# Queueing the first projection of each later stage inside the modulation loop, with split-weight refills one at a time behind it

## The reference

```python
def modulate(x, g, shift, scale):
    return rms_norm(x, g) * (1.0 + scale[:, None, :]) + shift[:, None, :]

# first block: attention + mLSTM, then a mixture of 32 experts
# second block, for i in range(2):
h = rmsnorm(x, norm1_g[i]) * (1.0 + scale1) + shift1
y = diff_attention(h, ...) if i == 0 else axial_gqa(h, ...)   # begins with h @ w_qkv
x = x + gate1 * y
h = rmsnorm(x, norm2_g[i]) * (1.0 + scale2) + shift2
x = x + gate2 * swiglu(h, f_w_in[i], f_w_out[i])              # begins with h @ w_in
```

## Time and profile before

| | us |
|---|---|
| median of 3 runs | 1378.43 (1378.06 to 1382.33) |
| profiled execution | 1377.22 |
| its span, first to last instruction | 1375.4 |
| TensorE busy | 1153.6 (84%) |
| VectorE busy | 611.5 (44%) |
| ScalarE busy | 540.8 (39%) |

### The profile page before, as it was taken

How to read it: one execution, slowest core, us unless ns; L and a number is a source line. 1 busy time by engine, 2 the same in 40 slices (tenths; PEclk the granted TensorE clock), 3 DMA queues, 4 the chain that set the end, 5 groups by cost and what they waited for, 6 DMA issues and landing times.

```text
span 1375.4 us, 22370 instructions
## 1 busy us (share of the span) xinstructions
PE 1153.6 (84%) x9627; PEld 917.0 (67%) x9627; DVE 611.5 (44%) x1363; ACT 540.8 (39%) x1203; POOL 0.2 (0%) x4
## 2 busy tenths in 40 slices
PE   6989998857475666657589989999999989999997
PEld 4867678534243443424257757999998758899997
DVE  4564664201110110101165765665555855655554
ACT  4554553211101111101155665555554654655553
POOL 0000000000000000000000000000000000000000
PEclk9999998989788889978899999999999999999999
DMA  9895847899999999999978655555546655655520
GB/s 390 345 356 223 355 186 294 341 427 427 428 426 426 424 427 427 426 426 428 426 299 307 235 194 198 231 184 184 185 153 230 228 215 184 245 184 184 184 93 31
DMA packets 29569, 397.53 MB, mean 289 GB/s; under 512 B 3480, under 2 KB 4888, under 8 KB 5400
## 3 DMA queue, kind: packets, MB, share of 16 engines
q1 hardware_dynamic: 29032, 395.72, 72.1%
q10 hardware_dynamic: 432, 0.30, 0.1%
HBM read 394.97 MB, written 1.05 MB: 288 GB/s over the span
## 4 chain that ended last, share of the span: by engine, by line
PE 61%; DMA 20%; DVE 10%; ACT 7%; issue 2%; SPq 0%; ACTq 0%; DVEq 0%
PE ps L141 61%; DMA mem<-in_w 13%; DMA ring<-in_w 5%; DVE mem L141 5%; DVE memr L141 3%; ACT mem L141 3%; ACT memr L141 3%; DMA ring<-in_wpk 1%; DVE small L141 1%; DMA posi<-in_pos 1%; ACT L141 0%; ACT rowb L141 0%; DVE x L141 0%; SPq L141 0%; DVE mcol L141 0%
## 5 line engine op out<-in xcount | busy, mean ns | idle before, releaser
L141 PE MATMUL ps<-memr 128*128 128x256 f32 (+1 forms) x4680 | 670.6, 303 | 17.9 <-DVE memr L141 17.9
L141 PEld LDWEIGHTS ps<-memr 128*128 128x128 f32 x4680 | 612.4, 193 | 62.5 <-DVE memr L141 27.8
L141 DVE TENSOR_TENSOR memr<-ring,memr 128x512 fp32r<-128x512 f32 x440 | 297.7, 690 | 247.0 <-ACT memr L141 243.6
L141 PE MATMUL ps<-mem 128*32 128x256 f32 (+5 forms) x2360 | 299.1, 421 | 86.8 <-DMA ring<-in_w 34.9
L141 ACT ACTIVATE memr<-ring 128x512 fp32r<-128x512 f32 x440 | 268.2, 627 | 221.6 <-PE ps L141 214.6
L141 PEld LDWEIGHTS ps<-mem 128*32 128x32 f32 (+3 forms) x2360 | 185.9, 150 | 158.6 <-issue 106.7
L141 ACT ACTIVATE mem<-ps 128x256 f32<-128x256 f32 (+5 forms) x307 | 121.3, 407 | 417.4 <-PE ps L141 415.4
L141 PE MATMUL ps<-ring,mem 128*32 128x256 f32 x1408 | 150.4, 428 | 40.5 <-DMA mem<-in_w 35.7
L141 DVE TENSOR_TENSOR mem<-mem,ps 128x256 f32<-128x256 f32 (+1 forms) x76 | 31.7, 418 | 270.3 <-ACT mem L141 270.3
L141 PEld LDWEIGHTS ps<-ring,mem 128*32 128x32 f32 x1408 | 72.8, 122 | 78.9 <-issue 53.3
L141 DVE COPY mem<-ps 32x256 f32<-32x256 f32 (+2 forms) x81 | 38.2, 471 | 118.7 <-PE ps L141 117.7
(11 more groups left out here) (91 smaller groups left out, 379.7 us busy)
## 6 DMA issues: line engine op xcount, KB each, us to landing
ring<-in_wpk SPq DMA_DIRECT2D x89, 2048.0 KB, 8.1
mem<-in_w SPq DMA_DIRECT2D x52, 2048.0 KB, 34.4
ring<-in_w SPq DMA_DIRECT2D x44, 2048.0 KB, 36.5
mem<-in_wpk SPq DMA_DIRECT2D x1, 2048.0 KB, 10.4
ring<-in_wpk SPq DMA_DIRECT2D x2, 1024.0 KB, 5.3
x<-in_x SPq DMA_DIRECT2D x2, 512.0 KB, 5.7
out_dram<-mem SPq DMA_DIRECT2D x4, 256.0 KB, 2.2
cst<-in_cst SPq DMA_DIRECT2D x1, 944.0 KB
```

What stands on the lines that cost most here:

```text
L141: ins = o[1](*o[2], **o[3])
```

## The change

The diff turns `project` into steps, as `project_T` was, and lets `modulate_x` queue them: after low(c) for c of 2 or more, one step of the projection is queued. Step k so follows low(k+2), and steps 0 to 5 are queued inside the loop. While a projection is begun, `stage` is called with 1: one slab per step. `slab()` no longer calls `stage` unless nothing is split. In the plain modulation before the experts the hold is lifted. The silu table is loaded where silu is first used.

```diff
         def slab():
-            stage()
+            if st["made"] == st["used"]:
+                stage(1 if begun else NSP)
@@
             sp_free[z] = [rec]
             st["used"] += 1
-            stage()
+            stage(1 if begun else NSP)
@@
-        def project(x2, x_r, evac, order=tuple(range(8))):
+        def project_steps(x2, x_r, out):
...
                 if kk == 2:
                     ada_close(True)
+                yield
+            out.extend([bk, r])
+
+        def project(x2, x_r, evac):
+
+            g, out = begun.pop(0) if begun else (None, [])
+            for _ in g or project_steps(x2, x_r, out):
+                pass
+            bk, r = out
@@ def low(c, z, sh, ra), in modulate_x(..., first=None)
                 uu_free[z] = [recs[c]]
+                if first:
+                    if c == 0:
+                        out = []
+                        begun.append((first(h2, recs, out), out))
+                    if c >= 2:
+                        next(begun[0][0])
@@
                 if plain:
+                    st["hold"] = False
@@
-                if split and 0 < c < 4:
-                    stage(1)
-                if c == 1 and not split:
+                if c == 1 and st["hold"]:
                     st["hold"] = False
                     stage()
+                elif st["used"] == st["made"] or (split and 0 < c < 4):
+                    stage(1)
@@ callers
-        h2_r = modulate_x(1, 0, rB_r, x1_r, {3: ada_copy}, scale=am1_r)
+        h2_r = modulate_x(1, 0, rB_r, x1_r, {3: ada_copy}, scale=am1_r, first=project_steps)
-            h2_r = modulate_x(i, 1, rB_r, x_r, {3: ada_copy})
-            use_tables(SILU)
+            h2_r = modulate_x(i, 1, rB_r, x_r, {3: ada_copy},
+                              first=lambda x2, recs, out: project_T_steps(x2, recs, 128, 256, out))
-                h2_r = modulate_x(2, 0, rB_r, x_r, {3: ada_copy})
+                h2_r = modulate_x(2, 0, rB_r, x_r, {3: ada_copy}, first=project_steps)
```

More of the change, by code:

```diff
@@ L324, in program @@
         side = []
+        begun = []
         def stage(most=NSP):
@@ L461, in mm3 @@
             return mm(out, a[1], b[0], False, stop)
-        def project(x2, x_r, evac, order=tuple(range(8))):
+        def project_steps(x2, x_r, out):
             bk = [PB.take(), PB.take()]
-            for kk, k in enumerate(order):
+            for kk, k in enumerate(range(8)):
                 w, ld, z = slab()
@@ L499, in project_T @@
         def project_T(x2, x_r, c1, c2):
-            out = []
-            for _ in project_T_steps(x2, x_r, c1, c2, out):
+            g, out = begun.pop(0) if begun else (None, [])
+            for _ in g or project_T_steps(x2, x_r, c1, c2, out):
                 pass
@@ L577, in gcol_of, with modulate_x @@
             return ([C_N1, C_N1B, C_N1B + 8] if half == 0 else [C_N2, C_N2B, C_N2B + 8])[i]
-        def modulate_x(i, half, rB_r, x_r, hooks={}, scale=None, plain=False, recs=None):
+        def modulate_x(i, half, rB_r, x_r, hooks={}, scale=None, plain=False, recs=None, first=None):
             held, frees = None, list(h2_free)
```

## The result

The changed kernel is slower. Its median is 1386.83 us (1382.53 to 1390.95, 8 runs), that of the kernel before in the same comparison 1378.59 (1377.14 to 1382.33, 8 runs). The ratio is 1.0043, 95% interval 1.0028 to 1.0058; the ratio alone means 5.9 us, the medians differ by 8.2. The profiled execution took 1382.53 us, its span is 1380.8, 5.4 more than before; it is the shortest of the eight and has the highest mean granted clock of them, 0.947 (the longest, 1390.95 us, has 0.939).

A forecast was written before the change was run, and what follows sets the result against it. TensorE, 61% of the chain, was taken as the bound, losing time where it waits. Terms 0.5 + 3.1 - 0.5 + 2.7 + 1.0 + 0.8 = +7.6 us on 1377.22 gave 1384.8, plus 1.2 for the median: 1386.0; range 1379.5 to 1390.

The forecast's parts named there:

- The period: Modulation loop: each chunk with a refill takes 2.18 us, a loop through two in-order engines; 0.79 without a refill.
- Feed-forwards: Both feed-forwards: step 4 at 9.35, step 7 at 16.09 us behind scale(0); -0.5 us in the first, +1.0 in the last.
- Second attention: i = 2, half 0: step 7 at 16.09 us behind scale(0) instead of 13.43; +2.7 us.
- Start of the second block: i = 1, half 0: one slab per period instead of four at chunk 1, step 7 at 17.96 instead of 14.89; +3.1 us.
- Split stage: i = 0, half 0: chunk 0 also calls for a slab ahead of scale(1); +0.5 us, bounds 0 and 0.5.
- The table: Silu table load before the first silu of each feed-forward: 0.4 us each, 0.8 in all; bounds 0 and 1.28 each.
- The sum: Whole kernel: all terms together add +7.6 us, giving a median of 1386.0 us.
- The waits: TensorE's waits for split operands: about 26 us in all instead of 17.9.
- The loop at engine rate: Rival, modulation loop: copies overlap, chunk period 1.41 us, stalls gone; -5.3 us, 1373; chance 0.10.
- taken back later: Rival, attention places: about 5.8 us of lateness vanishes in later waits, +1.8 left, 1380; chance 0.14.
- the falling clock: Rival, the stretches with refills: TensorE's clock falls, about 1.5 us each, two falls, 1389; chance 0.20.

The follow-up runs named there:

- experiment 4: Changed kernel with each refill's subtraction moved behind the next scale and low part, and four slabs split at chunk 1 (i = 1) again; 1373.72 us, ratio 0.9943.
- Experiment 3: Changed kernel with the projection begun early at the two feed-forwards only, both attention places as before; 1381.22 us, ratio 1.0002.
- experiment 2: Kernel before with one edit: the silu table loaded at first use, not behind the modulation loop; 1376.59 us, ratio 0.9963.
- experiment 5: Changed kernel with no refill inside the loop once a projection is begun, and four slabs split at chunk 1 (i = 1) again; 1386.74 us, ratio 1.0038.

## Why the prediction was right, point by point

- **The period.** Forecast 2.18 us per chunk where a refill is in the loop; measured 2.18. That it is the wait through both engines and not the work is shown by experiment 4: the same instructions, with the subtraction one chunk behind its copy, run at 1.39.
- **Feed-forwards.** Step 4 forecast at 9.35, measured 9.25; step 5 at 12.13 (from scale(6) at 11.10), measured 12.00. Step 7 forecast at 16.09, measured 15.98 and 15.97. The stall before step 4 went, and lateness grew from step 6 on. Against the kernel before step 7 is 0.8 later in the last feed-forward (forecast 1.0) and 0.65 earlier in the first (forecast 0.5).
- **Second attention.** Same positions (9.25, 12.00, 14.19, 15.97), as forecast. I gave +2.7 for the place. Step 7 before stood at 13.57, not at the 13.43 that I had worked out, so it is 2.4 later. Experiment 3 has 5.7 for both attention places, against 5.8, with the uncertainty given there.
- **Start of the second block.** Steps 0, 1, 5 and 7 forecast at 3.21, 6.20, 15.22 and 17.96; measured 3.21, 6.18, 15.30 and 18.15. The next place begins 3.2 us later than before, forecast 3.1.
- **Split stage.** Forecast +0.5 with bounds 0 and 0.5: TensorE's first step is at 3.21 instead of 2.73, but the matmuls behind step 3 start at 32.80 instead of 32.70. +0.1: the term was mis-sized. TensorE runs the four steps without idle in both, so a later start would come out whole at the same clock. But the granted clock, 0.50 from 24 us on in both, came back a little earlier in the changed kernel's execution (the microsecond from 29 to 30, before and then changed, shows 0.53 and 0.67), and fewer matmuls ran at the lower level. That is luck of these two executions, and whether the term is nearer 0.1 or 0.5 elsewhere is not shown.

```profile
29.00:30.00 1.00, 1.00 (x7) 1.00 (x7) 1.00 (x3) 0.18 (x1) 0.00 (x0) 0.53 0.96 410
```
```profile
29.00:30.00 1.00, 1.00 (x8) 1.00 (x8) 0.35 (x1) 1.00 (x3) 0.00 (x0) 0.67 0.77 328
```

- **The table.** Forecast 0.4 at each first silu. In the last feed-forward refill 16, which waits for step 12, starts at 1200.06, and refill 11, which waits for step 7, at 1192.49. That is 7.57; before, the same two were 7.26 apart (1187.50 and 1194.76). So 0.31. One load takes 1.28 us, the ScalarE row before it ends 0.02 ahead of it, and the next activation starts 1.29 behind its start (879.97 and 881.26), as in rows 3: no drain of 1.38 us on either side.

```profile
1192.49 0.63 ACT L141 ACTIVATE memr<-ring 128x512 fp32r<-128x512 f32 x1 [1.16 <-PE ps L141]
...
1200.06 0.63 ACT L141 ACTIVATE memr<-ring 128x512 fp32r<-128x512 f32 x1 [1.01 <-PE ps L141]
```

The figure of the Trainium skill (ScalarE: Activation LUTs, section What ACT_TABLE_LOAD costs) would have made some 2.8 more over the two feed-forwards, an estimate; the trace does not agree with it.

- **The sum.** 7.6 forecast. The profiled execution has +5.4 in span, and the medians +8.2. The forecast of 1386.0 lies within 1 us of the median, 1386.83, and that is in part luck: by the ratio the difference is 5.9, with an interval from 3.9 to 8.0. The profiled execution of before holds a second fall of the clock at 1101 to 1105 which I did not price; six matmuls that take 1.62 us in the changed kernel took 2.42 there. The lateness at i = 2 shows as only +1.0 one place later for that reason (3.1 to 4.1). From scale(0) to scale(0) the stretch took 108.73 us before and 109.68 in the changed kernel, but 107.09 and 107.11 in experiments 2 and 3, which queue that stretch as the kernel before does and show no fall in it. So the place costs 2.6, and the fall hid 1.6 of it.
- **The waits.** Forecast about 26 us for split operands, measured 22.3. The row of step 5 lasts 1.69 us, but at full speed the next step starts 1.44 after it: the idle that the trace gives is counted from the end of the row and leaves out the first 0.25 of each wait, and most of the short one before step 7 (0.09 shown, 0.35 lost). I had added up lateness and compared it with idle.
- **Rivals.** The loop at engine rate did not happen. Experiment 4 shows what it gives: 7.9 us under the kernel before by the ratio, where I had worked out 5.3; that its 1373.7 is so near my 1373 comes from the higher median of the kernel before in that comparison. The lateness was not taken back later. Of the falling clock, the profiled execution shows none. In the eight executions the time goes with the mean granted clock (1382.53 us at 0.947, 1387.64 at 0.944, 1390.95 at 0.939), so the spread is largely the clock's. It is no sign for this rival: the kernel before spreads in the same way (27 executions from 1377.32 at 0.944 to 1385.13 at 0.935), and where in the span the clock fell is on record for the profiled executions alone.
- **What the forecast did not see.** That the early queueing brings a wait of its own, through the sums of `ada_close` (I counted only their 0.6 us of work). In the changed kernel it is covered; experiment 5 shows it open, at 1.5 to 1.65 us per place.
- **What I had wrong about the cure.** I took experiment 4 for a copy moved ahead of high(c). By the traces ScalarE's order did not change; the subtraction moved.

## What to carry to other kernels

When work is moved from behind a loop into it, write out the order on each engine and look for a path that leaves an in-order engine and comes back to it within one iteration: the period is then the sum of the handovers (2.18 us here), not the busiest engine's share (1.39). The cure can be a few places in one queue: let the instruction that waits for the other engine come one iteration behind the instruction it waits for. And a step that is queued early takes all its instructions along, so count the waits among them.

## What the runs showed that I had not expected

- Times scatter by more than the places account for, and with them the mean granted clock: scale(0) of the second block stands at 696.2 us in the profiled execution of experiment 3 and at 701.3 in that of experiment 4, whose queues up to there do the same work. Positions within a place repeat to about 0.05 us where the clock is the same. A change of a few us is better read by positions than by a handful of times.
- The same idle is followed by the lower clock in one execution and not in another: TensorE is idle 1.87 us in the second attention before, in experiment 2 and in the changed kernel, and of these three the clock fell behind it in the kernel before alone.
- Small work in an engine's idle is free only in that idle: moving 0.79 us of transposes from ahead of step 4 to behind it cost 0.9 us at each of three places, though step 4 stood where it did.
